# Low-rank products of the second block as rounded matmuls, their weights as small tiles of the weight ring

## The reference

```
h = rmsnorm(x, norm_gain); z = h @ w_in_2             # r, k, v, low-rank columns, gates
sh = sh + shift_mu * (sh_prev - sh)                   # token shift
w_lr = f[..., 3*D_RWKV : 3*D_RWKV + 64];  a_lr = f[..., 3*D_RWKV + 64:]
ww = w0 + tanh(w_lr) @ w_up                           # (512 x 64) @ (64 x 512)
decay = exp(-exp(-softplus(-ww) - 0.5))
a = sigmoid(a0 + a_lr @ a_up)                         # (512 x 64) @ (64 x 512)
kk = k * k_k / max(norm(k * k_k), 1e-12);  k = k * (1 + (a - 1) * k_a)
```

## Time and profile before

| | us |
|---|---|
| median of 3 runs | 1435.91 (1435.88 to 1438.25) |
| the profiled execution | 1436.6 |
| its span, first to last instruction | 1435.3 |
| TensorE busy in the span | 1415.9 (99%) |
| VectorE, ScalarE busy | 870.1 (61%), 629.6 (44%) |
| TensorE's granted clock, mean | 0.997 of full speed |

### The profile page before, as it was taken

One profiled execution on the slowest core, in us unless ns is written; L12 is line 12 of the kernel. 1 busy time (PEld: TensorE's weight loads), 2 busy tenths in 40 slices (PEclk: granted clock), 3 DMA queues, 4 the chain that ended last, 5 costly groups with the idle time before them and its releaser, 6 DMA issues.

```text
span 1435.3 us, 25321 instructions
## 1 busy us (share of the span) xinstructions
PE 1415.9 (99%) x9999; PEld 1134.3 (79%) x9999; DVE 870.1 (61%) x1230; ACT 629.6 (44%) x984; POOL 214.1 (15%) x238
## 2 busy tenths in 40 slices
PE   8999999999999999999999999999999999999898
PEld 4788888888788888888878888888888777777676
DVE  3677777788445767765556432344445855665736
ACT  4566555556453424222234431234334454444435
POOL 0000000000047888920006000000000000000200
PEclk9999999999999999999999999999999999999999
DMA  9444334443446676543323333333333222212111
GB/s 338 120 131 140 111 112 138 125 119 116 133 117 184 169 213 183 161 131 91 100 77 91 101 103 98 94 90 101 95 103 97 81 72 57 61 54 70 47 43 59
DMA packets 272957, 162.47 MB, mean 113 GB/s; under 512 B 6333, under 2 KB 260674, under 8 KB 272842
## 3 DMA queue, kind: packets, MB, share of 16 engines
q1 hardware_dynamic: 267242, 158.19, 37.4%
q10 hardware_dynamic: 5600, 2.66, 0.7%
HBM read 158.54 MB, written 2.29 MB: 112 GB/s over the span
## 4 chain that ended last, share of the span: by engine, by line
PE 91%; DVE 4%; ACT 2%; issue 2%; POOL 0%; DVEq 0%; ACTq 0%; POOLq 0%
PE PS L667 24%; PE PS L669 22%; PE PS L668 22%; PE PS L846 1%; DVE Hl L1939 1%; PE PS L916 1%; PE PS L872 1%; PE PS L918 1%; PE PS L917 1%; PE PS L1136 1%; PE PS L1152 1%; PE PS L704 1%; PE PS L851 1%; PE PS L863 1%; PE PS L1144 1%
## 5 line engine op out<-in xcount | busy, mean ns | idle before, releaser
L667 PE MATMUL PS<-Hh,whi 128*128 128x512 f32 x1120 | 455.0, 406 | 0.8 <-ACT tmp L1397 0.3
L669 PE MATMUL PS<-Hh,wlo 128*128 128x512 f32 x1120 | 436.8, 390 | 0.0
L668 PE MATMUL PS<-Hl,whi 128*128 128x512 f32 x1120 | 436.8, 390 | 0.0
L1927 DVE TENSOR_TENSOR wlo<-raw,whi 128x1024 fp32r<-128x1024 f32 (+1 forms) x211 | 277.2, 1314 | 115.4 <-ACT whi L1348 114.8
L1348 ACT ACTIVATE whi<-raw 128x1024 fp32r<-128x1024 f32 (+1 forms) x211 | 221.2, 1049 | 166.2 <-PE PS L669 127.0
L667 PEld LDWEIGHTS PS<-Hh,whi 128*128 128x128 f32 x1120 | 210.3, 188 | 58.2 <-issue 14.2
L669 PEld LDWEIGHTS PS<-Hh,wlo 128*128 128x128 f32 x1120 | 210.2, 188 | 44.8
L668 PEld LDWEIGHTS PS<-Hl,whi 128*128 128x128 f32 x1120 | 210.6, 188 | 40.9 <-issue 1.7
L547 POOL TENSOR_TENSOR mbuf<-mbuf,cact 128x1024 f32<-128x1024 f32 x32 | 65.7, 2053 | 423.7 <-DMA mbuf<-in_w_mod_dram 420.0
L667 PE MATMUL PS<-YBh,whi 128*128 128x512 f32 x256 | 99.7, 389 | 0.0
L669 PE MATMUL PS<-YBh,wlo 128*128 128x512 f32 x256 | 99.6, 389 | 0.0
(11 more groups left out here) (414 smaller groups left out, 1980.0 us busy)
## 6 DMA issues: line engine op xcount, KB each, us to landing
raw<-in_w_in_dram SPq DMA_DIRECT2D x106, 512.0 KB, 4.0
raw<-in_w_ff_dram SPq DMA_DIRECT2D x64, 512.0 KB, 3.7
mbuf<-in_w_mod_dram SPq DMA_DIRECT2D x32, 512.0 KB, 3.9
wm<-in_w_mod_dram SPq DMA_DIRECT2D x8, 1024.0 KB, 9.6
crow<-cum_rows SPq DMA_DIRECT2D x32, 256.0 KB, 4.5
raw<-in_w_branch_ssm_dram SPq DMA_DIRECT2D x16, 512.0 KB, 3.5
erow<-exp_rows SPq DMA_DIRECT2D x24, 256.0 KB, 5.0
raw<-in_w_out_dram SPq DMA_DIRECT2D x10, 512.0 KB, 3.5
```

What stands on the lines that cost most here:

```text
L667: pe.matmul(bank[:, :], whi[s][:, k, :], xh[:, kk, :], start=kk == 0, stop=False)
L668: pe.matmul(bank[:, :], whi[s][:, k, :], xl[:, kk, :], start=False, stop=False)
L669: last = pe.matmul(bank[:, :], wlo[s][:, k, :], xh[:, kk, :], start=False, stop=t == end - 1 and k == (order or range(kt))[-1])
L1927: v.tensor_tensor(wlo[s][:, 0:kt, :], raw[s][:, 0:kt, :], whi[s][:, 0:kt, :].bitcast(F32), ALU.subtract).then_inc(s_wlo, 1)
```

## The change

The low-rank rows are split as the other activations are, but stacked: LRw holds the rounded tanh rows in partitions 0 to 63 and their remainder in 64 to 127; LRa holds its rounded rows in 64 to 127 and their remainder in 0 to 63. The 64 weight rows stand in both halves of a weight tile ("lu", f) of the ring, w_up_2 in its first 128 columns and a_up_2 in its second; so one matmul of `whi` and one of `wlo` against the 512 columns give all four products of the parts. The tile takes four small transfers of 64x128. "lu" 0 stands in the list ahead of ("v", 0), "lu" 1 to 3 ahead of ("k", f). In window 0 "da" has bank 5 and follows "dw" at once; TensorE waits there for `s_lr` 5 instead of 1.

```diff
-    names2 += [("LR", [P, T]), ("WU", [P, T]), ("PW", [P, T])]
+    names2 += [("LRw", [P, T], F32R), ("LRa", [P, T], F32R), ("PW", [P, T])]
...
+    rank = lambda name, f: A[name][0][:, f * 128:(f + 1) * 128]
+    LU = {}
     for n, m in ORDER2:
+        if (n, m) == ("v", 0) or n == "k" and m > 0:
+            weight(("lu", m), (rank("w_up_2", m), rank("a_up_2", m)))
+            LU[tile0[("lu", m)]] = m
         weight((n + "2", m), cols(W2, OFF2[n] + m * 128))
...
     def eighths(t):
-        return tiles[t].shape[1] * tiles[t].shape[2] // 128
+        return 2 if t in LU else tiles[t].shape[1] * tiles[t].shape[2] // 128
...
         turn(("dw", f), s_sgm, 2 * f + 1, 2)
-        turn(("da", f), s_sgm, 2 * f + 2, 2)
+        if f > 0:
+            turn(("da", f), s_sgm, 2 * f + 2, 2)
+        else:
+            ring[("da", 0)] = (BK[5], s_xr, 1)
...
             if t >= 3:
                 sp.wait_ge(s_wlo, t - 2)
+            if t in LU:
+                for i, up in enumerate(tiles[t]):
+                    for rows in (slice(0, 64), slice(64, 128)):
+                        sp.dma_start(raw[t % 3][rows, i, :], up).then_inc(s_raw[t % 3], 16)
+                return
...
-                sp.dma_start(Z["WU"][0:64, :], A["w_up_2"][0]).then_inc(s_par2, 16)
-                sp.dma_start(Z["WU"][64:128, :], A["a_up_2"][0]).then_inc(s_par2, 16)
...
-        def low_rank(f, q, name):
+        def low_rank(f, i, name):
             bank, fs, fv = ring[(name, f)]
+            t = tile0[("lu", f)]
+            rows = Z[("LRw", "LRa")[i]]
             pe.wait_ge(fs, fv)
-            pe.matmul(bank[:, :], Z["WU"][q:q + 64, f * 128:(f + 1) * 128], Z["LR"][q:q + 64, :],
-                      start=True, stop=True).then_inc(s_dw, 1)
+            pe.wait_ge(s_whi, t + 1)
+            pe.wait_ge(s_wlo, t + 1)
+            pe.matmul(bank[:, :], whi[t % 3][:, i, :], rows[:, :], start=True, stop=False)
+            pe.matmul(bank[:, :], wlo[t % 3][:, i, :], rows[:, :], start=False,
+                      stop=True).then_inc(s_tile if i else s_dw, 1)
...
-            late, apart = (21, 1) if f == 0 else (0, 4)
+            late, apart = (21, 0) if f == 0 else (0, 4)
...
-                    act.activation(Z["LR"][0:64, :], Z["LR"][0:64, :], ACTF.Tanh).then_inc(s_lr, 1)
+                    act.activation(Z["Tt"][0:64, :], Z["Tt"][0:64, :], ACTF.Tanh).then_inc(s_lr, 1)
+                    act.activation(Z["LRa"][64:128, :], Z["Tt"][64:128, :], ACTF.Copy).then_inc(s_lr, 1)
+                    act.wait_ge(s_lr, 2)
+                    act.activation(Z["LRw"][0:64, :], Z["Tt"][0:64, :], ACTF.Copy).then_inc(s_lr, 1)
...
(ScalarE; before, the else branch alone)
+                if tile0[(n + "2", m)] - 1 in LU:
+                    tile_steps(("lu", f), 3, 2)
+                    tile_steps((n + "2", m), 5, 4 if f == 0 else 2)
+                else:
+                    tile_steps((n + "2", m), KT, None if (f, i) == (0, 0) else 1 if f > 0 and i in (3, 4) else 2)
...
+                if f == 0 and s == 2:
+                    v.wait_ge(s_lr, 3)
+                    for rows, at, to in ((Z["LRw"], 0, 64), (Z["LRa"], 64, 0)):
+                        split_lo(rows[to:to + 64, :], Z["Tt"][at:at + 64, :], rows[at:at + 64, :]).then_inc(s_lr, 1)
...
(VectorE, likewise)
+                    tile_steps(("lu", f), 4, 3)
+                    tile_steps((n + "2", m), 4, 3)
```

More of the change, by code:

```diff
@@ L222, in eighths, with landed @@
     def eighths(t):
-        return tiles[t].shape[1] * tiles[t].shape[2] // 128
+        return 2 if t in LU else tiles[t].shape[1] * tiles[t].shape[2] // 128
+    def landed(t):
+        return 16 * sum(4 if i in LU else 1 for i in range(t % 3, t + 1, 3))
     def last_tile(name):
@@ L230, in build_program @@
     N_PAR2 = 16 * 11
-    N_BC, N_WS, N_W2 = N_PAR2 + 64, N_PAR2 + 80, N_PAR2 + 128
+    N_BC, N_WS, N_W2 = N_PAR2 + 64, N_PAR2 + 80, N_PAR2 + 96
     s_const, s_par, s_par2 = sem("s_const"), sem("s_par"), sem("s_par2")
@@ L1052, in prep @@
                         pe.wait_ge(s_par2, N_W2)
-                        pe.wait_ge(s_lr, 1)
+                        pe.wait_ge(s_lr, 5)
                     low_rank(f, 0, "dw")
                 if s == late + apart:
-                    low_rank(f, 64, "da")
+                    low_rank(f, 1, "da")
                 if s == (15 if f else 23):
@@ L1344, in hi @@
             kt = eighths(t)
-            act.wait_ge(s_raw[s], 16 * (t // 3 + 1))
+            act.wait_ge(s_raw[s], landed(t))
             if t >= 3:
@@ L1706, in low_rank @@
         def low_rank(f, i):
-            act.wait_ge(s_dw, 2 * f + i + 1)
+            if i == 0:
+                act.wait_ge(s_dw, f + 1)
+            else:
+                act.wait_ge(s_tile, last_tile(("lu", f)))
             act.wait_ge(s_rec, f)
@@ L1861, in act_program @@
             for i, (n, m) in enumerate(WINDOWS[f]):
-                tile_steps((n + "2", m), KT, None if (f, i) == (0, 0) else 1 if f > 0 and i in (3, 4) else 2)
+                if tile0[(n + "2", m)] - 1 in LU:
+                    tile_steps(("lu", f), 3, 2)
+                    tile_steps((n + "2", m), 5, 4 if f == 0 else 2)
+                else:
+                    tile_steps((n + "2", m), KT, None if (f, i) == (0, 0) else 1 if f > 0 and i in (3, 4) else 2)
             drain()
@@ L2420, in prep @@
                     scaled_out(("lr", 0))
-                    shift(("lr", 0), 12, Z["LR"])
+                    shift(("lr", 0), 12, Z["Tt"])
                     scaled_out(("k2", 0))
@@ L2663, in dve_program @@
             for i, (n, m) in enumerate(WINDOWS[f]):
-                tile_steps((n + "2", m), KT, None if (f, i) == (0, 0) else 1 if f > 0 and i == 3 else 4)
+                if tile0[(n + "2", m)] - 1 in LU:
+                    tile_steps(("lu", f), 4, 3)
+                    tile_steps((n + "2", m), 4, 3)
+                else:
+                    tile_steps((n + "2", m), KT, None if (f, i) == (0, 0) else 1 if f > 0 and i == 3 else 4)
             drain()
```

## The result

| | before | after |
|---|---|---|
| median | 1435.89 us (4 runs, 1435.05 to 1438.25) | 1444.35 us (4 runs, 1442.61 to 1445.33) |
| span of the profiled execution | 1435.3 | 1443.7 |
| TensorE's granted clock, mean | 0.997 | 0.992 |

The ratio is 1.0056, 95% interval 1.0045 to 1.0068: 8.5 us slower, against 9.9 forecast.

What follows compares the result with a forecast made beforehand. TensorE, busy 99% of the span, was taken as the bound. Window 0 +9.1, later products -4.1, later waits +1.5, clock +3.4 gave +9.9 us: 1446.5 from 1436.6, less 0.7 for the median, 1445.8; range 1441.5 to 1449.5.

Steps and rivals of the forecast that it cites:

- What bounds the kernel: Whole kernel: TensorE is busy 99% of the span, so only shortening its work or making it wait moves the end.
- First wait: Window 0, before (v, 0): its conversion comes late in the ScalarE and VectorE queues; TensorE starts at 1127.0, 6.0 us lost.
- Second wait: Window 0, before (gb, 0): its conversion stands behind two exponentials that wait for the scan and head sums; 4.9 us lost.
- Products in window 0: Tile (v, 0) with both low-rank products takes 6.55 us instead of 8.32, bank wait included; 1.75 us saved.
- The clock: TensorE's granted clock falls behind each of the two new stops, 1.7 us each; 3.4 us lost.
- Products in windows 1 to 3, less what is given back: Six low-rank products take 0.46 us each, 4.1 us saved; later waits in windows 2 and 3 lose 1.5.
- Tt 0.45 to 0.5 late, twice: Windows 2 and 3: hi of (v, f) comes ahead of Ww and Tt on ScalarE; 1.0 us lost in all.
- 0.5 where window 3 begins: Start of window 3: the late lo there is now that of (k, 3) itself, so TensorE waits; 0.5 us lost.
- The clock staying up: Rival: no fall of the clock behind the new stops, +6.5 us, 1442.4; chance 0.2 together with a single fall, 1444.1.
- the faster case: Rival: both conversions are done in time and only the products' saving counts; 1430 to 1431.6 us, chance 0.04.
- costs nothing: Window 0, wait for `s_lr` 5 before the products: reached at 1125.5, asked for at 1131.2, so no loss.
- The third stop in window 1: Rival: the 1.4 us margin at (k, 1) fails and window 1 waits too; 1447 to 1450 us, chance 0.12.

Runs made afterwards that it cites:

- e1: The changed kernel with the conversions of (v, 0) and (gb, 0) each in an earlier slot on ScalarE and VectorE; 1432.77 us.
- e3: The changed kernel with only (v, 0) converted early, (gb, 0) left at its late place; 1438.59 us.
- e4: The changed kernel with its small tiles loaded and converted but unread, and the old F32 products on unsplit rows; 1447.98 us.
- e5: The changed kernel with useless bf16 matmuls on TensorE, 24 before (v, 0) and 19 before (gb, 0); 1441.81 us.
- e6: e4 (old F32 products, small tiles unread) with the early conversions of e1; 1435.56 us.
- e7: e2 with (ua, 0) converted ahead of two exponentials on ScalarE, and masks ahead of sigmoid and scan on VectorE in windows 2 and 3; 1432.98 us.
- e8: The kernel before, unchanged, executed once more for a second profile; 1437.68 us.
- e2: e1 with the two low-rank products behind the sixth step of (v, 0) in place of the fifth; 1433.43 us.

## Why the prediction was right, and which terms were off

**What bounds the kernel** held: only TensorE's waits and work moved the end. No case but the slower one was near; 1444.35 lies in the range, 1441.5 to 1449.5.

**First wait.** Forecast 6.0 us, start at 1127.0; measured 5.57 later than before, at 1126.60. `lo` of ("v", 0) was forecast for 1125.71 and started at 1125.23, since the earlier part of this execution ran 0.4 us ahead. Read from the same tile ahead, the stop is 5.95: the sum over the queue (early by the small tile's 0.8 and the missing 0.26) was right to 0.1 us. e1 and e3 show that the place of the conversion is the cause.

**Second wait.** Forecast 4.9, measured 4.80 of idle and 4.9 in the distances of starts. The chain behind the head sums could be taken whole from the rows of before, which is why it came out so well. e3 has it alone.

**Products in window 0.** Forecast 1.75, measured 1.75. The reason given for it fell in part: e4 takes as long there with F32 products (8.44 against 8.38 us), so the 1.75 is won by the bank and the place of "da". The prediction had the wait for the bank in its sum but put no separate price on it.

**The clock.** Forecast 2 x 1.7, measured 1.8 and 1.7, and e5 shows it as a cost of its own: with TensorE kept at work, 1.00 throughout. The one row of a fall at the program's start was enough, though that fall is itself missing in five of the thirteen profiles. The rule named in the prediction from the Trainium skill ("TensorE: Matmul & The Clock Gate", section "What's actually happening") agrees with the 0.50 that the rows show in both stops. At this point, the start of ("k", 1), the forecast stood at 9.1 + 3.4 = 12.5; measured 12.11 and 0.4 from ahead of the block: 12.5.

**Products in windows 1 to 3, less what is given back.** Forecast -4.1 + 1.5 = -2.6; measured -1.63 in window 1, -0.57 in window 2, -0.19 in window 3 (8.50 to 8.31, behind the place of the vanished stop): -2.4. That the sum is right is luck, since both terms were too small. The six products of these windows saved 0.77 to 0.83 us each, 4.8 in all: the price of 1.05 us for those behind `rwkv`'s matmuls leaves out that the step behind such a product takes 0.34 us in place of 0.23 (in before, 1154.89 to 1155.23). And 2.4 us were given back: twice 1.0, and 0.3 where window 3 begins. The mechanism of the first was not the one named. The step "Tt 0.45 to 0.5 late, twice" failed. Tt came in time in window 2, its end at 1237.19 and the read at 1237.24:

```profile
1236.60 0.59 ACT L1831 ACTIVATE Tt<-PS 128x512 f32<-128x512 f32 x1
```

```profile
1237.24 0.69 PE L1171 MATMUL PS<-Ww,Tt 64*64 64x64 f32 x32
```

The loss is on VectorE, which the prediction followed only for `lo`: the masks RK and the copy KA. In window 2 RK stands behind the sigmoid and the scan, and ends 0.49 too late for a TensorE that arrives earlier:

```profile
1229.19 1.23 DVE L2459 TENSOR_TENSOR_SCAN wk<-rs,wk 128x512 f32<-128x512 f32 x1
...
1230.93 0.72 DVE L2564 COPY_PREDICATED RK<-msk,PS 128x512 f32<-128x512 uint8 x1
```

Why there: before, the slower F32 products themselves gave VectorE the time. e6, with F32 products, waits for neither and has 0.32 for Tt instead, the stop that the prediction named. Two products of 0.46 bring the masks' wait forward ahead of Tt's. e7 confirms that these waits stand in a row: with the one for RK gone, KA's is longer and Tt's appears (0.41 and 0.93 us in window 3). The "0.5 where window 3 begins" was 0.3: ("k", 3) moved by 0.26.

**What the sum lacked.** The stop of 1.12 us inside the group in window 2 was in the trace of before, and I took it as part of the kernel. It went with the change, 1.4 us in distances of starts; this is nearly the whole of the difference between 9.9 and 8.5. That it would go could not be read from one profile, but it could have stood in the range as a stop without a releaser. The third fall of the clock, 0.64 us in this profile (1.9 in e8), is not the change's: the first profile of before is one of the three without it.

**The rivals.** The clock staying up fell by the profile after, the faster case by e1's contrast: its condition (conversions in time) is what e1 makes, and e1 is then 1432.8, above the 1430 to 1431.6 given, where the wait for `s_lr` costs 1.25 us and that ahead of ("ua", 0) 0.86. The prediction said of the first that it "costs nothing"; that was right for the changed kernel alone. The third stop in window 1 did not come: VectorE's `lo` of ("k", 1) ended 3.4 us before TensorE began. The margin of 1.4 in the prediction left the clock out, whose falls held TensorE up by 3.5 us; in e5, without them, it is 1.5 us. On the price of true 32-bit, the Trainium skill ("FP8 and Floating Point Precision", section "TensorE Precision Notes") has four passes. By that, two F32 products of window 1 are 1.84 us against 0.92 now, 0.92 won; the measured 1.63 is more, and the trace decides.

## What to carry to other kernels

A new entry in a list that sets the order of loads and conversions moves every entry behind it to the next place; follow each moved conversion through its engine's queue and ask what it now stands behind, before counting what the entry itself saves. Here the rounding saved 2.8 to 3.6 us, the new place of "da" 1.7, and the two moved conversions cost 14.3 (by the starts 5.95 and 4.87, and 3.5 for the clock falling behind the stops); putting both back ahead of the work that they had slipped behind turned +8.5 into -3.4 us, and one more conversion into -4.2. When TensorE gets faster, look for the wait that comes up next in every window, in the order in which TensorE meets them, and expect each that is taken away to hand part or all of its time to the one behind (all of it in e2). And give a gain to the part of a change that makes it only after a run in which that part stands alone: in window 0 the bank had won what the rounding was credited with.
